# Seven block products for eight in the first two gated networks, with all seven remainders of a unit on GpSimd

## The reference

```
def swiglu(x, wg, wu, wd):
    return (jax.nn.silu(x @ wg) * (x @ wu)) @ wd
...
h = h + 0.5 * swiglu(rmsnorm(h, ffn1_norm[i]), ffn1_wg[i], ffn1_wu[i], ffn1_wd[i])
...
h = h + 0.5 * swiglu(rmsnorm(h, ffn2_norm[i]), ffn2_wg[i], ffn2_wu[i], ffn2_wd[i])
```

## Time and profile before

| | |
|---|---|
| median of 3 runs | 2104.66 us (2102.88 to 2106.46) |
| span of the profiled execution | 2100.9 us |
| instructions | 37982 |
| TensorE busy | 2065.8 us, 98% |
| VectorE, ScalarE, GpSimd busy | 41%, 34%, 43% |

### The profile page before, as it was taken

The page is one execution under the profiler, slowest core; times in us unless marked ns, Lnnn a source line. Parts: engine busy times, 40 slices in busy tenths (PEclk is TensorE's granted clock), DMA queues, the critical chain, the costliest instruction groups (busy, mean ns, idle before and its releaser), DMA issues.

```text
span 2100.9 us, 37982 instructions
## 1 busy us (share of the span) xinstructions
PE 2065.8 (98%) x15692; PEld 1788.4 (85%) x15692; DVE 854.1 (41%) x1254; ACT 717.4 (34%) x1085; POOL 907.5 (43%) x690
## 2 busy tenths in 40 slices
...
PEclk9999999999999999999999999999999999999999
...
DMA packets 152360, 179.03 MB, mean 85 GB/s; under 512 B 7109, under 2 KB 142766, under 8 KB 152254
## 3 DMA queue, kind: packets, MB, share of 16 engines
...
...
## 4 chain that ended last, share of the span: by engine, by line
PE 72%; issue 13%; POOL 8%; DVE 5%; ACT 2%; DMA 1%; SPq 0%; POOLq 0%; DVEq 0%; ACTq 0%
PE ps L2061 47%; PE ps L2202 11%; POOL wlo L734 8%; PE ps L2709 2%; PE ps L2472 1%; PE ps L2503 1%; PE ps L2483 1%; PE ps L2303 1%; DVE tmp L1396 1%; DMA raw<-in_ffn_wu 1%; DVE Q L1880 0%; DVE K L1883 0%; PE ps L2510 0%; PE ps L2610 0%; PE ps L2560 0%
## 5 line engine op out<-in xcount | busy, mean ns | idle before, releaser
L734 POOL TENSOR_TENSOR wlo<-raw,whi 128x512 fp32r<-128x512 f32 x630 | 841.8, 1368 | 1068.0 <-ACT whi L830 1067.9
L2061 PE MATMUL ps<-xh,whi 128*128 128x258 f32 (+2 forms) x2400 | 687.3, 333 | 1.0 <-POOL wlo L734 0.7
L2061 PE MATMUL ps<-xh,wlo 128*128 128x258 f32 (+2 forms) x2400 | 682.0, 331 | 0.0
L2061 PE MATMUL ps<-xl,whi 128*128 128x258 f32 (+2 forms) x2400 | 680.3, 330 | 1.4 <-issue 1.4
L830 ACT ACTIVATE whi<-raw 128x2048 fp32r<-128x2048 f32 (+1 forms) x158 | 301.3, 1907 | 770.0 <-PE ps L2061 479.3
L2061 PEld LDWEIGHTS ps<-xh,whi 128*128 128x128 f32 x2400 | 406.7, 189 | 52.5 <-issue 3.1
L2061 PEld LDWEIGHTS ps<-xh,wlo 128*128 128x128 f32 x2400 | 405.6, 188 | 45.3 <-issue 1.9
L2061 PEld LDWEIGHTS ps<-xl,whi 128*128 128x128 f32 x2400 | 405.4, 189 | 45.4 <-issue 1.6
L2202 PE MATMUL ps<-act_h,wlo 128*128 (+1 forms) x528 | 208.6, 395 | 0.0
L2202 PE MATMUL ps<-act_l,whi 128*128 (+1 forms) x528 | 208.6, 395 | 0.0
L2202 PE MATMUL ps<-act_h,whi 128*128 (+1 forms) x528 | 208.6, 395 | 0.0
...
## 6 DMA issues: line engine op xcount, KB each, us to landing
...
```

Of the source, the lines that this page charges most:

```text
L734: last = nc.gpsimd.tensor_tensor(wlo[:, slot, d], raw[:, slot, d], whi[:, slot, d].bitcast(F32), ALU.subtract)
L2061: last = mm(ps[:, j * banks + b, 0:n], w[:, k, e * P:(e + 1) * P], x[:, k, c0:c0 + n], start=(k == 0 and q == 0), stop=(k == KD - 1 and q ...
```

## The change

The opening units stay. The twenty gate and up units behind them in each network are computed as products of 2 x 2 blocks: the weight unit is cut into two halves of the inner length by two tiles of columns, the input into the same two halves by two halves of the tokens (256 each). Seven block products of 4 slices by 3 matmuls of 256 columns, some of them on sums of blocks, give what eight give directly. Both kinds of sums have to be made in float32 and split again into a rounded part and a remainder:

- of the input once per network: eight scaled copies `xf` on ScalarE, four sums of 1024 elements on VectorE (`x_sums`), rounded on ScalarE (`sums_rounded`), remainders on VectorE (`x_rests`). They stand between the squares and the norm's root on both engines.
- of the weights in each unit: four sums of 512 on VectorE (`seven_sum`), written where the low part will lie; seven roundings of 512 on ScalarE (`seven_hi`); seven remainders of 512 on GpSimd (`seven_lo`), so that VectorE's `seven_rest` has nothing to do.

`whi` and `wlo` become a ring of eight pieces of 512 instead of two slots. A unit takes seven pieces, and a piece is freed by the product that used it (`seven_done`). Three partial results are copied out of PSUM by ScalarE (`kept`) and put together by VectorE (`seven_taken`): four additions and one scaling of 1024. Silu, product and remainder go over pairs of tiles. Since the input's sums take the room of the products' second half, each network becomes ten such units, six down units, whose result is added to h (`half_added`), ten more such units, five down units.

Names in the diff: f is the network, u a unit, j the piece or product 0 to 6, k the number of the unit among the twenty, v that number over both networks. Semaphores that two places can share are merged, which the diff below leaves out.

```diff
+PIECE = UNIT // 4
+PIECES = 2 * UNIT // PIECE
+HI_ORDER = (0, 3, 1, 2, 4, 5, 6)
+LO_ORDER = (0, 3, 1, 2, 4, 5, 6)
+SUMS = (1, 2, 4, 5)
...
+        self.kinds = ["open"] * 2 + ["seven"] * 10 + ["down"] * 6 + ["seven"] * 10 + ["embed"] * embed + ["down"] * 5
...
+            for j in range(7 if k == "seven" else 4):
+                self.at[first + o, j] = pos
+                self.user[pos] = (first + o, j)
+                pos += 1
...
+    def before(self, u, j):
+        return self.user[self.at[u, j] - PIECES]
...
+            def seven_lo(f, u):
+                for j in LO_ORDER:
+                    if j in (1, 4):
+                        pool.wait_ge(piece_sum, PIECE_SUM[u, SUMS[SUMS.index(j) + (2 if j == 1 else 1)]])
+                    pool.wait_ge(*rounded_piece(f, u, j))
+                    src = raw_block(u, *RAW_OF[j]) if j in RAW_OF else block_of(wsum_f, f, u, j)
+                    nc.gpsimd.tensor_tensor(block_of(wlo_f, f, u, j), src, block_of(whi_f, f, u, j).bitcast(F32),
+                                            ALU.subtract).then_inc(lo_ready if j == LO_ORDER[-1] else piece_lo, 1)
...
-            lo_run(4, W_IN1 + 1)
-            lo_run(W_IN1 + 1, GATE_UNIT)
+            ffn_lo(FFNS[0], 2, FFNS[0].end)
+            lo_run(W_IN1, GATE_UNIT)
...
+            def xf_of(n, gain):
+                nc.scalar.activation(xf[:, n, :], h[:, n, M:T], ACT.Copy, scale=col(gain, n)).then_inc(xf_ready, 1)
+
+            def sums_rounded(f):
+                act.wait_ge(sum_made, 16 * f.g + 4)
+                for i in range(4):
+                    nc.scalar.activation(sumh[:, i], sums[:, i], ACT.Copy).then_inc(xf_ready, 1)
...
+            def seven_period(f, k):
+
+                u = f.sevens[k]
+                i = (k + 2) // 2 if k % 2 else k // 2
+                more = f.kind(u + 1) == "seven"
+                d = f.downs[0 if k < 10 else 6]
+                if more:
+                    seven_hi(f, u + 1, 0)
+                kept(f, k, 0)
+                if not more and f.kind(u + 1) == "down":
+                    down_hi(f, d, 0)
+                kept(f, k, 1)
+                if more:
+                    seven_hi(f, u + 1, 3)
+                elif f.kind(u + 1) == "down":
+                    down_hi(f, d, 1)
+                else:
+                    embed_hi(f, u + 1)
+                if k % 2:
+                    silu_pair(f, (k + 1) // 2)
+                if more:
+                    seven_hi(f, u + 1, 1)
+                    seven_hi(f, u + 1, 2)
+                if k % 2 == 0 and k not in (0, 10):
+                    acth_pair(f, k // 2)
+                kept(f, k, 2)
+                if more:
+                    for j in (4, 5, 6):
+                        seven_hi(f, u + 1, j)
+
...
+                xf_of(n, "ffn1_norm")
+            sums_rounded(FFNS[0])
+            for j in (0, 3, 1, 2):
+                seven_hi(FFNS[0], 2, j)
...
+            def seven_sum(f, u, j):
+
+                out_ = block_of(wsum_f, f, u, j)
+                dve.wait_ge(*freed(f, u, j))
+                if j == 1:
+                    dve.wait_ge(raw_in[u % 2], raw_count(u))
+                    x, y, op = raw_block(u, 0, 1), raw_block(u, 1, 1), ALU.add
+                elif j == 2:
+                    x, y, op = raw_block(u, 0, 0), raw_block(u, 0, 1), ALU.subtract
+                elif j == 4:
+                    dve.wait_ge(piece_sum, PIECE_SUM[u, 1])
+                    x, y, op = block_of(wsum_f, f, u, 1), raw_block(u, 0, 0), ALU.subtract
+                else:
+                    dve.wait_ge(piece_sum, PIECE_SUM[u, 4])
+                    x, y, op = raw_block(u, 1, 0), block_of(wsum_f, f, u, 4), ALU.subtract
+                nc.vector.tensor_tensor(out_, x, y, op).then_inc(piece_sum, 1)
...
+                part = lambda row, half: xf[:, 4 * row:4 * row + 4, half * HS:(half + 1) * HS]
+                t = [sums[:, i] for i in range(4)]
+                n0 = 16 * f.g
+                dve.wait_ge(xf_ready, (KD + 4) * f.g + KD)
+                nc.vector.tensor_tensor(t[0], part(0, 1), part(0, 0), ALU.subtract).then_inc(sum_made, 1)
+                nc.vector.tensor_tensor(t[1], part(1, 1), part(0, 1), ALU.subtract).then_inc(sum_made, 1)
+                dve.wait_ge(sum_made, n0 + 1)
+                nc.vector.tensor_tensor(t[2], part(1, 1), t[0], ALU.subtract).then_inc(sum_made, 1)
+                dve.wait_ge(sum_made, n0 + 3)
+                nc.vector.tensor_tensor(t[3], part(1, 0), t[2], ALU.subtract).then_inc(sum_made, 1)
...
+            def seven_taken(f, k):
+
+                v = 20 * f.g + k
+                u = f.sevens[k]
+                b, q = 4 * (v % 2), sc[:, v % 2]
+                dst = tmp[:, 2:4, 0:S] if k % 2 else tmp[:, 0:2, M:T]
+                dve.wait_ge(seven_kept, 3 * v + 2)
+                nc.vector.tensor_tensor(q[:, 1, :], q[:, 1, :], q[:, 2, :], ALU.add).then_inc(seven_step, 1)
+                dve.wait_ge(seven_done, 6 * v + 4)
+                nc.vector.tensor_tensor(dst[:, 0, 0:HS], ps[:, b + 1, 0:HS], q[:, 0, :], ALU.add).then_inc(seven_step, 1)
+                dve.wait_ge(seven_kept, 3 * v + 3)
+                dve.wait_ge(tiles_done, used_count(u))
+                s0 = dst[:, 0, HS:HS + 1]
+                cross = bass.AP(tensor=s0.tensor, offset=s0.offset, ap=[s0.ap[0], [T - HS, 2], [1, HS]])
+                nc.vector.tensor_tensor(cross, ps[:, b + 2:b + 4, 0:HS], q[:, 3, :].unsqueeze(1).to_broadcast([P, 2, HS]), ALU.add).then_inc(seven_step, 1)
+                dve.wait_ge(seven_step, 4 * v + 1)
+                nc.vector.tensor_tensor(dst[:, 1, HS:S], q[:, 1, :], q[:, 3, :], ALU.add).then_inc(seven_step, 1)
+                dve.wait_ge(seven_step, 4 * v + 4)
+                nc.vector.tensor_tensor(dst, dst, rbs[:, M:T].unsqueeze(1).to_broadcast([P, 2, S]), ALU.mult).then_inc(up_scaled if k % 2 else gate_scaled, 2)
+
+            def prod_pair(f, i):
+                dve.wait_ge(gate_done, FT * f.g + 2 * i + 2)
+                dve.wait_ge(up_scaled, FT * f.g + 2 * i + 2)
+                nc.vector.tensor_tensor(tmp[:, 2:4, 0:S], tmp[:, 0:2, M:T], tmp[:, 2:4, 0:S], ALU.mult).then_inc(prod_done, 2)
+
+            def actl_pair(f, i):
+                t = 2 * i % UPS[0]
+                dve.wait_ge(acth_done, FT * f.g + 2 * i + 2)
+                nc.vector.tensor_tensor(actl2[:, t:t + 2, :], tmp[:, 2:4, 0:S], acth2[:, t:t + 2, :].bitcast(F32), ALU.subtract).then_inc(actl_done, 2)
...
+            x_sums(FFNS[0])
+            for j in (1, 2):
+                seven_sum(FFNS[0], 2, j)
+            x_rests(FFNS[0])
-            ffn_up(0, W_UP1)
+            ffn(FFNS[0])
...
+            def seven(f, k, made, embed=None):
+
+                u, v = f.sevens[k], 20 * f.g + k
+                b = 4 * (v % 2)
+                if k < 2:
+                    pe.wait_ge(gate_scaled, FT * f.g + 2)
+                    pe.wait_ge(up_scaled, FT * f.g + 2)
+                    made()
+                elif k in (10, 11):
+                    pe.wait_ge(sum_made, 16 * f.g + 8 + 4 * (k - 9))
+                else:
+                    pe.wait_ge(seven_step, 4 * (v - 1))
+                x_part = lambda row, half: [x[:, 4 * row:4 * row + 4, M + half * HS:M + (half + 1) * HS] for x in X]
...
+                moving = (x_part(0, 0), s_part(0), s_part(1), x_part(1, 0), s_part(2), x_part(1, 1), s_part(3))
...
+                for j in range(7):
+                    pe.wait_ge(*split_piece(f, u, j))
...
+                    if j in (4, 5):
+                        pe.wait_ge(seven_kept, 3 * v + j - 3)
+                    wh, wl = block_of(whi_f, f, u, j), block_of(wlo_f, f, u, j)
+                    xs = moving[j]
+                    out_ = ps[:, b + (0, 2, 3, 1, 0, 2, 3)[j], 0:HS]
+                    for c in range(4):
+                        for q, (w, x) in enumerate(((wh, xs[0]), (wl, xs[0]), (wh, xs[1]))):
+                            last = mm(out_, w[:, c, :], x[:, c, :], start=(j < 4 and c == 0 and q == 0), stop=(c == 3 and q == 2),
+                                      skip_group_check=True)
+                    if j < 6:
+                        last.then_inc(seven_done, 1)
+                    else:
+                        last.then_inc(tiles_done, 2)
```

533 lines of the change are left out of this document (412 added, 121 removed).

## The result

The changed kernel takes 2196.97 us (median of 4 runs, 2196.5 to 2201.57) against 2104.48 for the kernel before in the same session: a ratio of 1.0441, 95% interval 1.0426 to 1.0457. The forecast was 2210, its own range 2185 to 2240.

A forecast was written before the change was run, and what follows sets the result against it. TensorE alone was taken to bound the kernel before, GpSimd's and VectorE's turns the changed units. 76 + 21.6 + 2.5 + 2.4 + 4 = +106 us gave about 2210; own range 2185 to 2240, wider range 2155 to 2275.

The forecast's parts named there:

- The unit: Seven-product units: GpSimd and VectorE take turns, 13.0 us a unit as floor, 13.6 taken, against 11.12 before.
- VectorE's holds: In each unit, VectorE's two-SBUF-input operations keep GpSimd off, 0.46 us at 512 elements, 1.01 at 1024, 0.2 at 256.
- The sum over units: Forty changed units: 268 pieces x 13.6 / 7 = 520.7 us against 444.8 before, +76 us.
- the 12 pieces of credit: At starts of runs, some two of 70 pieces ready after an opening, four after down units; 268 pieces count.
- TensorE's pace: TensorE's 84 matmuls of 256 columns a unit would take 10.05 to 10.21 us, less than 11.12 before.
- TensorE's pace holds: Rival for the forty units: they cost TensorE's 10.2 us, ending at 2098, or 2092 with 10.05; chance 0.07.
- The first opening: First network's opening: x's sums and ten DMA issues (3.4 us) delay the root; first unit at 59.1, +21.6 us.
- Second opening: Second network's opening: spread slips by 1 us at most, second up tile's chain ends at about 757.7, +2.4 us.
- clock: After the first opening's idle time, matmuls run at 1.2 GHz until the clock rises again, about +2.5 us.
- down units: First down unit's first pieces queue behind the last unit's seven: 1 us, four times, +4 us.
- part collides: Rival for the units: 11.5 to 13 us each if 256-element additions cost nothing, 2130 to 2170; chance 0.1.
- whole waits: Rival, whole waits or whole holds: units of 14.8 us give 2256, of 15.4 give 2280; chance 0.2.

The follow-up runs named there:

- 5 to 2: Against the changed kernel, the remainders of two of a unit's seven pieces go from GpSimd to VectorE; 2185.88 us.
- 4 to 3: Against the changed kernel, the remainders of pieces 2, 4 and 5 of a unit go from GpSimd to VectorE; 2172.78 us.
- e5: Against the changed kernel, GpSimd subtracts half of each piece and TensorE uses that half's remainders twice, so the output is wrong; 2086.87 us.
- e1: Against the changed kernel, the first opening's root stands right behind the squares, with VectorE's reciprocal before the sums of x; 2195.94 us.
- e6: Against the changed kernel, root first in the first opening, and all four tiles scaled before x's remainders and the products in both openings; 2199.66 us.

## Why the prediction held, step by step

**The unit.** Predicted 13.0 as a floor and 13.6 taken; 13.21 measured. The make-up was a little different. GpSimd's seven subtractions last 12.1 us (117.7 / 68 = 1.73 each, 806 to 930 us), so over the base of 8.75 VectorE's holds take 3.4 of a unit and not 4.26; waiting, most of it for sums, takes the other 1.1 and not 0.6. VectorE's sums last 1.78 us, a little over the 1.1 to 1.7 named as a sign. The number was met more closely than the theory deserves: a floor made of GpSimd's turns alone was 52 us off for 5 to 2 (2134 against 2185.88) and some 65 for 4 to 3, because VectorE's sum is as large. With seven remainders on GpSimd the two sums happen to meet.

The lock that the Trainium skill states (page "SBUF — State Buffer", section "SBUF: two separate sides") agrees here in that VectorE's operations with two SBUF inputs and GpSimd's exclude each other and PSUM reads (674 ns) are free of it. Held for the whole of each instruction it would have made 14.8 us a unit, and 13.21 with GpSimd's waiting in it says that less than the whole is held.

**The sum over units.** The step predicted 268/7 units of 13.6, 520.7 us. Measured against e5's 9.80 the forty units took 392 + 112 = 504, so +59 instead of **+76**: 17 us too much, of which 38 x 0.39 = 15 is the unit time. The first three units of each run go at 10.9, which saves 28 us over the four runs; the 12 pieces of credit had it at 23.

**TensorE's pace.** Predicted 10.05 to 10.21, measured 9.80 where nothing holds it back (e5), 116.7 ns a matmul. The rival "TensorE's pace holds" would have ended at 2087, not 2092 to 2098.

**The first opening.** +21.6 predicted, +17.5 measured. The mechanism was right, with a wrong term: the ten DMA issues, 3.4 us. In the timeline of ScalarE they stand beside its roundings and delay nothing:

```profile
36.70 0.28 ACTq L1232 DMA_DIRECT2D rows_t<-in_mix_norm  x1
...
39.77 0.28 ACTq L1232 DMA_DIRECT2D rows_t<-in_hgrn_norm_w  x1
...
41.48 1.28 ACT L1020 ACT_TABLE_LOAD   x1
42.77 0.27 ACT L1020 ACTIVATE std<-ps,epsc 128x4 f32<-128x4 f32 x1
```

The root is made at 42.77, not after 47; the spread followed at 43.30, not 47.6. (By its own terms the prediction's root is at 42.9 + 3.4 + 1.28 = 47.6, not 47.3.) The kernel before already showed the issues beside ScalarE's work: they begin at 25.16 in the earlier trace rows, and the rounding that stands ahead of them in the program began only then:

```profile
25.62 1.90 ACT L830 ACTIVATE whi<-raw 128x2048 fp32r<-128x2048 f32 x1
```

From the spread to the first unit it is 11.7 us, where 11.5 were predicted. e1 and e6 add that most of the price stays wherever the root stands.

**Second opening, clock, down units.** +2.4 against 3.8 measured, of which 0.6 has come before the opening's first unit. The spread slips by 2.5 us, not by 1, and not because of the root: TensorE stands still for 2.0 us, to 791.89, until GpSimd's four remainders are made beside VectorE's sums of x, in 7.92 us where they took 5.04 in the earlier trace rows:

```profile
783.92 7.92 POOL L870 TENSOR_TENSOR wlo<-raw,whi 128x512 fp32r<-128x512 f32 x4 [8.28 <-ACT whi L1001]
```

Another 1.35 us ahead of the first unit is put down to issue. So the size was about right and the path was another. The clock's part stands in TensorE's rows: its first unit begins after 5.5 us of idle time, the granted clock is 0.51 (1.2 GHz) between 55 and 60 us and 1.00 (2.4 GHz) in the next 5, and 23 intervals of 0.21 us instead of 0.117 cost 2.3 us, near the predicted +2.5. Clock, down units and the other first units together come to 6.7 in e5 (its networks gain 46.1 us on before, where 40 x 1.32 would be 52.8), which leaves about 4 for the rest, as predicted for the down units.

**What was not foreseen.** The 6.6 us of instruction stops. Without them the prediction's sum of 106 stands against 87: the units' 17 and the opening's 4 too much were hidden in part by this omission, which is luck. The rivals: "part collides" (2130 to 2170) and "whole waits" (2256, 2280) lie outside what was measured.
